# A Fourier mixing branch computed as even and odd halves, with the value projection moved ahead of it

## The chip, the cores and the metric

The kernel runs on one core of one Trainium2 chip. The metric is the device time of one execution in microseconds. The engines are named as the profile names them: PE is TensorE's matrix multiplication, PEld its weight load, DVE is VectorE, ACT is ScalarE, POOL is GpSimd and SP is SyncE, which issues most of the transfers here.

## The reference

The whole program is a hybrid mixer block, a cross attention and a feed-forward block, followed by a second block of two layers with adaptive norms. Everything is fp32, with 256 tokens of width 1024 (and 256 context tokens beside them). The change touches one place: the mixer of the first layer of the second block, which runs on both streams, x and context.

```python
def fourier_mix(a):                       # a: 256 tokens x 512
    a4 = a.reshape(b_, n, FOURIER_GROUPS, FOURIER_CH)     # 4 groups of 128 channels
    f = jnp.fft.fftn(a4, axes=(1, 3), norm="ortho").real  # over tokens and channels
    return f.reshape(b_, n, D_FOURIER)

def chunk_sgu(u, v, g_v, w_s, b_s):       # 4 groups of 128 channels, chunks of 128 tokens
    vh = rms_norm(v.reshape(b_, n, SGU_GROUPS, SGU_CH), g_v)
    vc = vh.reshape(b_, n // CHUNK_2, CHUNK_2, SGU_GROUPS, SGU_CH)
    mixed = jnp.einsum('hpq,bcqhd->bcphd', w_s, vc) + b_s.T[None, None, :, :, None]
    return u * mixed.reshape(b_, n, D_SGU)

def fourier_sgu_mixer(h, w_in, g_v, w_s, b_s, w_out):
    a, uv = jnp.split(h @ w_in, [D_FOURIER], axis=-1)
    u, v = jnp.split(jax.nn.gelu(uv), 2, axis=-1)
    return jnp.concatenate([fourier_mix(a), chunk_sgu(u, v, g_v, w_s, b_s)], axis=-1) @ w_out
```

## The kernel before, in words

The program is a chain of projections whose weights are streamed from memory, one chunk of at most 1 MB (128 partitions by 2048 numbers) at a time, in the order of a list called `plan`. SP loads chunks into three slots of `raw`. ACT copies a chunk to a reduced-precision `w_hi` (L234), DVE subtracts to get the rest `w_lo` (L242), and PE multiplies in three passes (L258, L259, L260), high by high, high by low and low by high. A chunk's loads and splits run two chunks ahead of PE. The activations are split in the same way into `xn_hi` and `xn_lo`. A second stream, 72 chunks of the adaptive norm's weights (`mods`), is multiplied by `mods_pe` (L1589) in places that a table, `MODS_BEHIND`, names; three of them (24 matmuls) belong to the stage of this change.

Both streams, 512 tokens, go through the branch together. Its projections are `ab_a` (the Fourier input), `ab_u` and `ab_v` (the gate and the value of the gating half), two chunks each, and then `ab_out`, four chunks. Between the last of the first three and `ab_out` lies what is called the Fourier stage here. It works on eight pieces j, one for each of four groups and two streams:

- `channels(j)` (L1731) multiplies by `dft_c`, cosine and minus sine side by side, 256 columns, two matmuls for the two halves of the tokens;
- ACT copies the 512 results to `mid` (L1772);
- four matmuls (L1743, L1744) multiply by the tokens' `dft_cos` and `dft_sin`, 256 columns each, into one sum;
- DVE copies the 256 results to `o_t` (L1811).

`channels(j + 1)` is issued ahead of the token matmuls of j. The value has to be normed before it is mixed over tokens: DVE squares and sums it (L1798, L1799), ACT makes a reciprocal root (L1767), DVE scales it (L1805, L1808), and PE mixes (L1749) after the eight pieces. Then come the three chunks of `mods`. Last, the branch's results are made ready for `ab_out`: the Fourier half is split by one ACT copy of 2048 numbers (L1774) and one DVE subtraction (L1815), the gated half is summed (L1823), multiplied (L1824) and split (L1778, L1815). `ab_out` starts when all of this but the last subtractions is done, by the line `pe.wait_ge(g_dve, 12)`. These are the waits ahead of the stage and in front of `ab_out`:

```python
            pe.wait_ge(evacuated, jobs["ab_v"].base + 2)
            ...
            pe.wait_ge(g_dve, 12)
            def branches_k(s, k):
                if s.c == 0 and k in (0, 4, 6):
                    pe.wait_ge(o_lo, max(1, k // 2))
```

All order on each engine is written out by hand, and engines wait for each other through counting semaphores.

Of the kernel before, what the change touches and what calls it, by code (L numbers as in the profile page):

```python
# [41 lines left out]
ACT = mybir.ActivationFunctionType  # L42
ALU = mybir.AluOpType
AX_X = mybir.AxisListType.X

P = 128
# [32 lines left out]
    "a1_down1": {0: (1, 1), 1: (1, 1), 2: (1, 1), 3: (1, 1), 5: (1, 1), 7: (3, 2)},  # L79
    "ab_v": {1: (3, 2)},  # L80
    "ab_out": {3: (3, 2)},
# [47 lines left out]
def build(nc, io, plan):  # L129
# [23 lines left out]
    with ExitStack() as ctx:  # L153
        def sb(name, shape, dt=F32, scope=ctx):
            return scope.enter_context(nc.sbuf_tensor(name, shape, dt))
# [105 lines left out]

        def pe_feature_major(pe, job, act_hi, act_lo, span, n_tiles=2, k_tiles=KT, before_k=None, after_chunk=None):


            for s in steps(job):
                bank_free(pe, s)
                pe.wait_ge(lo_ready, s.g + 1)
                for k in range(k_tiles):
                    if before_k is not None:
                        before_k(s, k)  # L270
                    for n in range(1 if packed(s) else n_tiles):
                        w = slice((n * k_tiles + k) * P, (n * k_tiles + k + 1) * P)
# [1435 lines left out]
        GATING = (4, 5, 0, 1)  # L1708
        o_t = area(0, KT, 2 * T)
# [7 lines left out]

        def branch_pe(pe, norm, turn):
            pe_feature_major(pe, jobs["ab_a"], xn_hi, xn_lo, XC, before_k=norm.ready_at_first(pe))
            turn()  # L1720
            pe_feature_major(pe, jobs["ab_u"], xn_hi, xn_lo, XC)
            pe_token_major(pe, jobs["ab_v"], XC)
            pe.wait_ge(evacuated, jobs["ab_v"].base + 2)
            pe.wait_ge(l0_tables_in, 16 * len(L0_TABLES))

            def channels(j):
                q, g = j // 4, j % 4
                if j >= 2:
                    pe.wait_ge(f_mid_out, j - 1)
                for nt in range(2):  # L1730
                    mm = pe.matmul(psum[:, j % 2, nt * T:(nt + 1) * T], a_t[:, g, q * T + nt * P:q * T + (nt + 1) * P], dft_c[:, :],  # L1731
                                   start=True, stop=True)
                mm.then_inc(f_mid, 1)

            channels(0)
            for j in range(8):
                if j + 1 < 8:
                    channels(j + 1)
                pe.wait_ge(f_mid_out, j + 1)
                if j >= 2:  # L1740
                    pe.wait_ge(f_sum_out, j - 1)
                for nt in range(2):
                    pe.matmul(psum[:, 2 + j % 2, 0:T], mid[j % 2][:, nt, 0:P], dft_cos[:, nt, :], start=(nt == 0), stop=False)  # L1743
                    mm = pe.matmul(psum[:, 2 + j % 2, 0:T], mid[j % 2][:, nt, P:T], dft_sin[:, nt, :], start=False, stop=(nt == 1))  # L1744
                mm.then_inc(f_sum, 1)
            pe.wait_ge(g_dve, 8)
            for tt in range(4):
                for g in range(4):
                    mm = pe.matmul(psum[:, GATING[g], tt * P:(tt + 1) * P], v_t[:, tt, g * P:(g + 1) * P], ws_t[:, g, :], start=True, stop=True)  # L1749
            mm.then_inc(g_pe, 1)  # L1750
            mods_pe(pe, mods_behind("ab_v", 1))
            pe.wait_ge(g_dve, 12)

            def branches_k(s, k):
                if s.c == 0 and k in (0, 4, 6):
                    pe.wait_ge(o_lo, max(1, k // 2))
            pe_feature_major(pe, jobs["ab_out"], xn_hi, xn_lo, XC, before_k=branches_k)

        def branch_act(act, norm, then):
            norm.act_rest(act)  # L1760
            for name in L0_TABLES:
                act.dma_start(L0_TABLES[name][:], io[name]).then_inc(l0_tables_in, 16)
            run_act(act, jobs["ab_a"], act_copy_to(act, a_t, w=2 * T), counts=True)
            run_act(act, jobs["ab_u"], act_copy_to(act, u_t, ACT.Gelu_apprx_tanh, w=2 * T), counts=True)
# [3 lines left out]
            for j in range(8):  # L1768
# [3 lines left out]
                act.activation(mid[j % 2], psum[:, j % 2, :].rearrange("p (n t) -> p n t", n=2), ACT.Copy).then_inc(f_mid_out, 1)  # L1772
            act.wait_ge(f_sum_out, 8)
            act.activation(xn_hi[:, 0:4, :], o_t[:, 0:4, :], ACT.Copy).then_inc(o_hi, 1)  # L1774
            for i in range(2):
                act.wait_ge(g_dve, 10 + 2 * i)
                k = slice(4 + 2 * i, 6 + 2 * i)
                act.activation(xn_hi[:, k, :], o_t[:, k, :], ACT.Copy).then_inc(o_hi, 1)  # L1778
            run_act(act, jobs["ab_out"], then.act_squares_after(act))

        def branch_dve(dve, norm, rows_out, columns):
# [3 lines left out]
            columns()  # L1785
            for name in ("ab_u", "ab_v"):
                run_dve(dve, jobs[name], None)
            n = 0
# [19 lines left out]
            o(dve.tensor_tensor(v4, v4, gv, ALU.mult))  # L1808
            for j in range(8):
                dve.wait_ge(f_sum, j + 1)  # L1810
                dve.tensor_copy(o_t[:, j % 4, (j // 4) * T:(j // 4 + 1) * T], psum[:, 2 + j % 2, 0:T]).then_inc(f_sum_out, 1)  # L1811
# [5 lines left out]
            low(0, slice(0, 4))  # L1817
            dve.wait_ge(g_pe, 1)
            for i in range(2):
                k = slice(4 + 2 * i, 6 + 2 * i)  # L1820
                gated = o_t[:, k, :].rearrange("p g (n t) -> p g n t", t=P)
                bs = bs_row[:, 2 * i:2 * i + 2, :].unsqueeze(2).to_broadcast([P, 2, 4, P])
                o(dve.tensor_tensor(gated, psum[:, GATING[2 * i]:GATING[2 * i] + 2, :].rearrange("p g (n t) -> p g n t", t=P), bs, ALU.add))  # L1823
                o(dve.tensor_tensor(o_t[:, k, :], o_t[:, k, :], u_t[:, 2 * i:2 * i + 2, :], ALU.mult))  # L1824
            for i in range(2):
                low(1 + i, slice(4 + 2 * i, 6 + 2 * i))
            run_dve(dve, jobs["ab_out"], dve_add_gated(dve, 2, gate_of(1), 2))
# [576 lines left out]
def shape_tables():  # L2404
# [218 lines left out]
```

## Time and profile before

| | |
|---|---|
| median of 3 runs | 2249.84 us (2249.29 to 2254.49) |
| the profiled execution's own time | 2254.1 us |
| its span | 2252.3 us |
| PE busy | 2133.1 us, 95% of the span |
| DVE, ACT, POOL busy | 1001.3, 791.9, 224.7 us |
| mean granted clock of PE | 0.982 of full |

An engine's busy time is that in which it executes something. The chain of waits is followed back from the last instruction, at each step to what released it. An fp32 matmul whose operands are not in reduced precision stands in the trace as two records, so the eight pieces' 32 token matmuls with `dft_cos` and `dft_sin` are 64 records. The record of a matmul begins before the one ahead of it has ended, since they are pipelined; the distance between two ends is the cost.

### The profile page before, as it was taken

The page shows a single profiled execution, that of the slowest core. Times are in us where ns is not written, and L with a number is a line of the kernel's source. Part 1 is how long each engine was busy: PE and PEld are TensorE (multiplying, and loading weights), DVE is VectorE, ACT ScalarE, POOL GpSimd, SP SyncE. Part 2 cuts the span into 40 slices and gives each one's busy share as a digit, 9 for nine tenths or more (in the row PEclk, how much of TensorE's full clock was granted, in tenths as well). Part 3 has the DMA queues.
Part 4 walks back from the last instruction along what each step waited for, and adds up shares of the span by engine and source line. Part 5 has one row for each costly group of instructions (what it writes and reads, how often), then busy time and mean ns, then how long its engine had stood idle before and what let it go on. Part 6 is the DMA issues. An engine that isn't in the chain of part 4 may idle for free.

```text
span 2252.3 us, 30888 instructions
## 1 busy us (share of the span) xinstructions
PE 2133.1 (95%) x13477; PEld 1809.1 (80%) x13477; DVE 1001.3 (44%) x1286; ACT 791.9 (35%) x969; POOL 224.7 (10%) x185
## 2 busy tenths in 40 slices
PE   6988998999999999999999999999999998989997
PEld 6985897999788888778768788877877886858997
DVE  6668554767522321353452232234223235645444
ACT  5642353555422222232232222233212223434443
POOL 1000000413111011100101101110100110001111
PEclk9999999999999999999999999999999999999999
DMA  6425454454531333451334332234234222363553
GB/s 227 150 77 211 166 185 187 152 185 161 196 144 65 112 128 115 171 199 57 112 134 165 103 112 85 83 129 165 107 133 159 82 78 98 113 242 135 175 178 104
DMA packets 53688, 314.23 MB, mean 140 GB/s; under 512 B 5936, under 2 KB 12081, under 8 KB 23729
## 3 DMA queue, kind: packets, MB, share of 16 engines
q1 hardware_dynamic: 51360, 309.51, 38.3%
q10 hardware_dynamic: 2192, 2.75, 0.4%
q8 instruction: 106, 1.74, 0.3%
q14 instruction: 30, 0.24, 0.0%
HBM read 311.19 MB, written 1.05 MB: 139 GB/s over the span
## 4 chain that ended last, share of the span: by engine, by line
PE 85%; DVE 9%; ACT 4%; issue 2%; DMA 1%; SPq 0%; DVEq 0%; ACTq 0%
PE psum L258 26%; PE psum L259 25%; PE psum L260 25%; PE psum L1589 2%; DVE w_lo L242 2%; ACT w_hi L234 2%; PE psum L1268 1%; PE psum L1246 1%; DVE work L407 1%; PE psum L1260 0%; PE psum L1743 0%; PE psum L1744 0%; DMA raw<-in_w_in_r 0%; DVE work L695 0%; ACT work L1280 0%
## 5 line engine op out<-in xcount | busy, mean ns | idle before, releaser
L258 PE MATMUL psum<-xn_hi,w_hi 128*128 128x256 f32 (+1 forms) x2504 | 849.1, 339 | 35.6 <-DVE xn_lo L416 15.7
L259 PE MATMUL psum<-xn_lo,w_hi 128*128 128x256 f32 (+1 forms) x2504 | 842.2, 336 | 0.0
L260 PE MATMUL psum<-xn_hi,w_lo 128*128 128x256 f32 (+1 forms) x2504 | 841.6, 336 | 0.0
L242 DVE TENSOR_TENSOR w_lo<-raw,w_hi 128x2048 fp32r<-128x2048 f32 (+1 forms) x246 | 509.9, 2073 | 420.2 <-ACT w_hi L234 419.4
L258 PEld LDWEIGHTS psum<-xn_hi,w_hi 128*128 128x128 f32 x2504 | 483.3, 193 | 99.1 <-issue 42.9
L260 PEld LDWEIGHTS psum<-xn_hi,w_lo 128*128 128x128 f32 x2504 | 482.8, 193 | 47.2
L259 PEld LDWEIGHTS psum<-xn_lo,w_hi 128*128 128x128 f32 x2504 | 483.2, 193 | 46.3 <-issue 0.7
L234 ACT ACTIVATE w_hi<-raw 128x2048 fp32r<-128x2048 f32 (+1 forms) x246 | 421.6, 1714 | 194.0 <-PE psum L260 157.2
L258 PE MATMUL psum<-h_hi,w_hi 128*128 128x512 f32 (+1 forms) x880 | 309.2, 351 | 1.7 <-POOL h_lo L1564 1.7
L259 PE MATMUL psum<-h_lo,w_hi 128*128 128x512 f32 (+1 forms) x880 | 307.7, 350 | 0.0
L260 PE MATMUL psum<-h_hi,w_lo 128*128 128x512 f32 (+1 forms) x880 | 307.7, 350 | 0.0
L1564 POOL TENSOR_TENSOR h_lo<-work,h_hi 128x512 fp32r<-128x512 f32 (+1 forms) x110 | 154.7, 1407 | 1171.9 <-ACT h_hi L1497 1171.9
L1535 DVE TENSOR_TENSOR work<-work,psum 128x512 f32<-128x512 f32 (+1 forms) x88 | 54.7, 621 | 407.7 <-ACT work L1486 407.7
L1486 ACT ACTIVATE work<-psum 128x512 f32<-128x512 f32 (+1 forms) x88 | 47.9, 544 | 514.4 <-PE psum L260 514.3
L258 PEld LDWEIGHTS psum<-h_hi,w_hi 128*128 128x128 f32 x880 | 165.5, 188 | 29.7 <-issue 4.1
L260 PEld LDWEIGHTS psum<-h_hi,w_lo 128*128 128x128 f32 x880 | 165.5, 188 | 23.9
L259 PEld LDWEIGHTS psum<-h_lo,w_hi 128*128 128x128 f32 x880 | 165.5, 188 | 23.5
L1421 DVE SCALAR_TENSOR_TENSOR xc<-psum,mods,xc 128x256 f32<-128x256 f32 x136 | 59.9, 480 | 235.1 <-PE psum L260 234.9
L343 POOL TENSOR_TENSOR work<-work 128x256 f32<-128x256 f32 (+1 forms) x60 | 62.2, 1037 | 763.2 <-ACT work L334 712.8
L334 ACT ACTIVATE work<-xc 128x512 f32<-128x512 f32 (+2 forms) x48 | 30.3, 632 | 228.8 <-DVE xc L1421 202.3
L1589 PE MATMUL psum<-raw,c_pad 128*32 128x256 f32 x1152 | 77.9, 391 | 11.7 <-DMA raw<-in_mod 11.7
L1497 ACT ACTIVATE h_hi<-work 128x512 fp32r<-128x512 f32 (+1 forms) x110 | 60.1, 547 | 78.7 <-DVE work L1535 78.7
(341 smaller groups left out, 1321.8 us busy)
## 6 DMA issues: line engine op xcount, KB each, us to landing
raw<-in_mod SPq DMA_DIRECT2D x72, 1024.0 KB, 4.8
raw<-in_a_up SPq DMA_DIRECT2D x42, 1024.0 KB, 4.8
raw<-in_b_up SPq DMA_DIRECT2D x42, 1024.0 KB, 4.8
raw<-in_ffn_up SPq DMA_DIRECT2D x22, 1024.0 KB, 5.1
raw<-in_a_down SPq DMA_DIRECT2D x32, 704.0 KB, 4.1
raw<-in_b_down SPq DMA_DIRECT2D x32, 704.0 KB, 4.2
raw<-in_ffn_down SPq DMA_DIRECT2D x16, 704.0 KB, 4.1
raw<-in_wo SPq DMA_DIRECT2D x8, 1024.0 KB, 4.8
```

What stands on the lines that cost most here:

```text
L234: act.activation(w_hi[:, slot, 0:size], raw[:, raw_slot(("main", g)), 0:size], ACT.Copy).then_inc(hi_ready, 1)
L242: dve.tensor_tensor(w_lo[:, slot, 0:size], raw[:, raw_slot(("main", g)), 0:size], w_hi[:, slot, 0:size].bitcast(F32), ALU.subtract).then_i ...
L258: pe.matmul(out, lh, rh, start=first, stop=False, skip_group_check=group)
L259: pe.matmul(out, lh, rl, start=False, stop=False, skip_group_check=group)
L260: return pe.matmul(out, ll, rh, start=False, stop=last, skip_group_check=group)
L343: pool.tensor_tensor(nrm[:, 0, 0:self.w], nrm[:, 0, 0:self.w], nrm[:, k, 0:self.w], ALU.add).then_inc(n_added, 1)
L1421: mm = dve.scalar_tensor_tensor(x, got, gate[:, tile, h], x, ALU.mult, ALU.add)
L1486: act.activation(b[r, 0, 0:self.w], psum[r, s.bank, 0:self.w], ACT.Silu).then_inc(ff_gate, 1)
L1497: act.activation(out, b[r, 1:2, 0:self.w], ACT.Copy).then_inc(ff_hi, 1)
L1535: dve.tensor_tensor(b[r, 1, 0:self.w], b[r, 0, 0:self.w], up[up_r], ALU.mult).then_inc(evacuated, 1)
L1564: pool.tensor_tensor(lo, b[r, 1:2, 0:self.w], hi.bitcast(F32), ALU.subtract).then_inc(ff_lo, 1)
L1589: mm = pe.matmul(psum[q, 7, 0:256], c_pad[:, k, C_AT - 2 * j:C_AT - 2 * j + 32], raw[:, raw_slot(("mod", m)), k * 256:(k + 1) * 256], star ...
```

## The change

The Fourier transform of real input is symmetric. The change computes half of each transform and makes the other half from it.

- Over channels, only the cosines of 0 to 64 and the sines of 1 to 63 are multiplied, 128 columns for 256. ACT makes both full rows of `mid` from them with four activations for the one of before: the cosine half, the sine half, and the mirror image of each, written with a step of -1 (the sine's with scale -1).
- Over tokens, cosine and sine sums are kept apart, 129 columns each for 256. ACT copies the sine sum to SBUF (`odd_out`), and DVE writes sum and difference of the two (`halves`), the difference with a step of -1 in output and ascending input.
- `ab_v` is projected ahead of `ab_u`, so the value's norm is computed beside `ab_u`'s matmuls. PE no longer waits for the last evacuation of the projections before the stage, only for the one before it.
- The gating matmuls are cut in two parts of 8 (after pieces 1 and 4) and the three `mods` chunks are put singly after pieces 2, 4 and 6.
- The split of the results is cut from three groups to six (each Fourier group as it comes), and `ab_out` takes its k tiles in the order 0, 1, 4, 5, 2, 6, 7, 3, each waiting only for its own.

```diff
@@ pe_feature_major
-                for k in range(k_tiles):
+                for k in k_order:
@@ tables
+        GATED_BANK, MID_BANK, TOKEN_BANK = 0, 2, 4
+        OUT_ORDER = (0, 1, 4, 5, 2, 6, 7, 3)
+        OUT_READY = {0: 1, 1: 2, 4: 3, 2: 4, 6: 5, 3: 6}
@@ branch_pe
+            pe_token_major(pe, jobs["ab_v"], XC)
             pe_feature_major(pe, jobs["ab_u"], xn_hi, xn_lo, XC)
-            pe_token_major(pe, jobs["ab_v"], XC)
-            pe.wait_ge(evacuated, jobs["ab_v"].base + 2)
+            pe.wait_ge(evacuated, jobs["ab_u"].base + 1)
...
+            def tokens(j):
+                pe.wait_ge(f_mid_out, j + 1)
+                if j >= 2:
+                    pe.wait_ge(f_sum_out, 2 * j - 2)
+                for nt in range(2):
+                    pe.matmul(psum[:, TOKEN_BANK + j % 2, 0:P + 1], mid[j % 2][:, nt, 0:P], dft_cos[:, nt, :], start=(nt == 0), stop=(nt == 1))
+                for nt in range(2):
+                    mm = pe.matmul(psum[:, TOKEN_BANK + j % 2, T:T + P + 1], mid[j % 2][:, nt, P:T], dft_sin[:, nt, :], start=(nt == 0), stop=(nt == 1))
+                mm.then_inc(f_sum, 1)
...
             for j in range(8):
                 if j + 1 < 8:
                     channels(j + 1)
+                tokens(j)
+                if j == 1:
+                    gating(0)
+                if j == 4:
+                    gating(1)
+                if j in (2, 4, 6):
+                    mods_pe(pe, 1)
@@ branch_act
+            def middle(j):
+                act.wait_ge(f_mid, j + 1)
+                if j >= 2:
+                    act.wait_ge(f_sum, j - 1)
+                got, m, h = psum[:, MID_BANK + j % 2, 0:T].rearrange("p (n t) -> p n t", n=2), mid[j % 2], P // 2
+                act.activation(m[:, :, 0:h + 1], got[:, :, 0:h + 1], ACT.Copy)
+                act.activation(m[:, :, P + 1:P + h], got[:, :, h + 1:P], ACT.Copy)
+                act.activation(m[:, :, P - 1:h:-1], got[:, :, 1:h], ACT.Copy)
+                act.activation(m[:, :, 2 * P - 1:P + h:-1], got[:, :, h + 1:P], ACT.Copy, scale=-1.0).then_inc(f_mid_out, 1)
...
+            def odd_out(j):
+                act.wait_ge(f_sum, j + 1)
...
+                act.activation(odd_half[j % 2], psum[:, TOKEN_BANK + j % 2, T:T + P + 1], ACT.Copy).then_inc(f_odd, 1)
...
+            middle(0)
+            for j in range(3):
+                middle(j + 1)
+                odd_out(j)
+            fourier_high(0)
@@ branch_dve
+            def halves(j):
+                dve.wait_ge(f_odd, j + 1)
+                g, t = j // 2, j % 2 * T
+                even, odd = psum[:, TOKEN_BANK + j % 2, 0:P + 1], odd_half[j % 2]
+                dve.tensor_tensor(o_t[:, g, t:t + P + 1], even, odd, ALU.add).then_inc(f_sum_out, 1)
+                dve.tensor_tensor(o_t[:, g, t + T - 1:t + P:-1], even[:, 1:P], odd[:, 1:P], ALU.subtract).then_inc(f_sum_out, 1)
```

On PE, at the start of the Fourier stage, this is what stood there before: two `channels`, then four token matmuls and two channel matmuls for each piece, all with 256 columns, and at the end the gating and the `mods` in one block each.

```order
L1731 MATMUL psum<-dft_c,a_t 128x256 x4
L1743 MATMUL psum<-dft_cos,work 128x256
L1744 MATMUL psum<-dft_sin,work 128x256
L1743 MATMUL psum<-dft_cos,work 128x256
L1744 MATMUL psum<-dft_sin,work 128x256
...
L1749 MATMUL psum<-ws_t,v_t 128x128 x16
L1589 MATMUL psum<-raw,c_pad 32x256 x24
L258 MATMUL psum<-xn_hi,w_hi 128x512
```

On PE the stage of the changed kernel begins as follows; L1735 is `channels`, L1744 and L1746 are `tokens`, L1756 is `gating`.

```order
L1735 MATMUL psum<-dft_c,a_t 128x128 x4
L1744 MATMUL psum<-dft_cos,work 128x129 x2
L1746 MATMUL psum<-dft_sin,work 128x129 x2
L1735 MATMUL psum<-dft_c,a_t 128x128 x2
L1744 MATMUL psum<-dft_cos,work 128x129 x2
L1746 MATMUL psum<-dft_sin,work 128x129 x2
L1756 MATMUL psum<-ws_t,v_t 128x128 x8
L1735 MATMUL psum<-dft_c,a_t 128x128 x2
L1744 MATMUL psum<-dft_cos,work 128x129 x2
L1746 MATMUL psum<-dft_sin,work 128x129 x2
L1589 MATMUL psum<-raw,c_pad 32x256 x8
```

The matmuls are as many as before but half as wide, and half of the gating and a `mods` chunk have moved in between pieces.

On ACT, around the same place, these rows stood before: the last evacuations of the projections (L1393 is u, L1405 is v), the root of the norm, the eight copies of the middle, and the splits.

```order
L1393 ACTIVATE u_t<-psum 128x1024
L234 ACTIVATE w_hi<-raw 128x2048
L1405 ACTIVATE v_t<-psum 128x4x256
L234 ACTIVATE w_hi<-raw 128x2048
L1405 ACTIVATE v_t<-psum 128x4x256
L1767 ACT_TABLE_LOAD
L1767 ACTIVATE work<-work 128x16
L1772 ACTIVATE work<-psum 128x512 x8
L1774 ACTIVATE xn_hi<-work 128x2048
```

And these stand there on ACT in the changed kernel, down to the first `odd_out` (L1811).

```order
L1405 ACTIVATE v_t<-psum 128x4x256
L1785 ACT_TABLE_LOAD
L1785 ACTIVATE work<-work 128x16
L234 ACTIVATE w_hi<-raw 128x2048
L1393 ACT_TABLE_LOAD
L1393 ACTIVATE u_t<-psum 128x1024
L234 ACTIVATE w_hi<-raw 128x2048
L1393 ACTIVATE u_t<-psum 128x1024
L1793 ACTIVATE work<-psum 128x2x65
L1794 ACTIVATE work<-psum 128x2x63
L1795 ACTIVATE work<-psum 128x2x63
L1796 ACTIVATE work<-psum 128x2x63
```

The root and its table load have moved ahead of the evacuation of u, one more table load stands before that evacuation, and one more stands at the next norm (ahead of L361), since the root's table is no longer the last one loaded.

## Rows read from the trace of the kernel before

**Rows 1.** The page: span, busy shares, and the chain that ended last, by engine.

```profile
span 2252.3 us, 30888 instructions
PE 2133.1 (95%) x13477; PEld 1809.1 (80%) x13477; DVE 1001.3 (44%) x1286; ACT 791.9 (35%) x969; POOL 224.7 (10%) x185
PE 85%; DVE 9%; ACT 4%; issue 2%; DMA 1%; SPq 0%; DVEq 0%; ACTq 0%
```

**Rows 2.** Stretches of time: length, busy us of each engine, granted clock, DMA.

```profile
1047.40:1085.80 38.40, 30.26 (x177) 25.12 (x176) 20.36 (x21) 10.05 (x13) 0.00 (x0) 0.91 0.10 37
1053.00:1059.70 6.70, 5.51 (x13) 4.38 (x14) 5.90 (x8) 1.19 (x3) 0.00 (x0) 0.50 0.00 0
1059.70:1076.00 16.30, 16.30 (x77) 14.34 (x77) 2.55 (x6) 3.58 (x6) 0.00 (x0) 1.00 0.00 1
1085.80:1091.00 5.20, 5.17 (x16) 4.10 (x17) 4.65 (x3) 2.87 (x2) 0.00 (x0) 0.67 0.80 336
```

**Rows 3.** PE in order of time: start, us, line, count, idle time before.

```profile
1047.15 0.28 PE L260 MATMUL psum<-w_hi,xn_lo 128*128 128x256 f32 x1
1048.60 1.99 PE L1731 MATMUL psum<-dft_c,a_t 128*128 128x256 f32 x8 [1.17 <-ACT v_t L1405]
1054.19 1.22 PE L1743 MATMUL psum<-dft_cos,work 128*128 128x256 f32 x2 [3.60 <-ACT work L1772]
...
1079.63 2.80 PE L1589 MATMUL psum<-raw,c_pad 128*32 128x256 f32 x48
1085.83 0.50 PE L258 MATMUL psum<-xn_hi,w_hi 128*128 128x512 f32 x1 [3.40 <-DVE work L1824]
```

**Rows 4.** The chain of waits, in order of time: start, us, what.

```profile
1061.45 0.86 PE psum L1731 x4
1062.32 0.43 PE psum L1743 x2
```

**Rows 5.** The gating matmuls' line: count, ns, first and last start.

```profile
L1749 PE MATMUL psum<-ws_t,v_t x32: 273/275/275, 1076.0 to 1079.4; 128*128 128x128 f32 x32
```

**Rows 6.** ACT in order of time, from the last projection to the splits.

```profile
1047.53 1.02 ACT L1405 ACTIVATE v_t<-psum 128x1024 f32<-128x1024 f32 x1 [8.69 <-PE psum L260]
1048.57 1.28 ACT L1767 ACT_TABLE_LOAD   x1
1053.44 0.22 ACT L1767 ACTIVATE work<-work 128x16 f32<-128x16 f32 x1 [3.59 <-DVE work L1800]
1053.56 1.07 ACT L1772 ACTIVATE work<-psum 128x512 f32<-128x512 f32 x2
1076.63 1.91 ACT L1774 ACTIVATE xn_hi<-work 128x2048 fp32r<-128x2048 f32 x1 [3.32 <-DVE work L1811]
```

**Rows 7.** Groups by line and shape, ACT copies from PSUM and small DVE operations.

```profile
L1486 ACT ACTIVATE work<-psum 128x256 f32<-128x256 f32 x21 | 8.1, 385 | 56.2 <-PE psum L260 56.2
L1772 ACT ACTIVATE work<-psum 128x512 f32<-128x512 f32 x8 | 4.7, 594 | 15.1 <-PE psum L1731 15.1
L791 DVE COPY s<-psum 128x128 f32<-128x128 f32 x1 | 0.3, 284 | 0.0
```

**Rows 8.** DVE in order of time, in the stage and after it.

```profile
1048.58 2.29 DVE L1798 TENSOR_TENSOR work<-v_t 128x2048 f32<-128x2048 f32 x1 [7.42 <-ACT v_t L1405]
...
1056.72 2.29 DVE L1808 TENSOR_TENSOR v_t<-v_t,gv_row 128x2048 f32<-128x2048 f32 x1
...
1076.17 0.42 DVE L1811 COPY work<-psum 128x256 f32<-128x256 f32 x1 [1.30 <-PE psum L1744]
1098.74 1.66 DVE L1421 SCALAR_TENSOR_TENSOR xc<-psum,mods,xc 128x256 f32<-128x256 f32 x4 [7.74 <-PE psum L260]
1109.61 1.66 DVE L1421 SCALAR_TENSOR_TENSOR xc<-psum,mods,xc 128x256 f32<-128x256 f32 x4 [3.98 <-PE psum L260]
```

**Rows 9.** ACT in order of time, at the norm behind `ab_out`.

```profile
1133.06 1.06 ACT L334 ACTIVATE work<-xc 128x1024 f32<-128x1024 f32 x1 [8.01 <-DVE xc L1421]
1138.19 0.63 ACT L363 ACTIVATE rstd<-mean 128x512 f32<-128x512 f32 x1 [3.98 <-DVE mean L384]
```

More of the change, by code:

```diff
@@ L79 @@
     "a1_down1": {0: (1, 1), 1: (1, 1), 2: (1, 1), 3: (1, 1), 5: (1, 1), 7: (3, 2)},
-    "ab_v": {1: (3, 2)},
+    "ab_u": {1: (3, 2)},
     "ab_out": {3: (3, 2)},
@@ L1707, in build @@
         L0_TABLES = dict(dft_c=dft_c, dft_cos=dft_cos, dft_sin=dft_sin, ws_t=ws_t, bs_row=bs_row, gv_row=gv_row)
-        GATING = (4, 5, 0, 1)
+        GATED_BANK, MID_BANK, TOKEN_BANK = 0, 2, 4
+        odd_half = [work[:, 5120 + i * T:5120 + i * T + P + 1] for i in range(2)]
+        f_odd, f_clear = sem("fourier_odd_half"), sem("fourier_zeros")
+        OUT_ORDER = (0, 1, 4, 5, 2, 6, 7, 3)
+        OUT_READY = {0: 1, 1: 2, 4: 3, 2: 4, 6: 5, 3: 6}
         o_t = area(0, KT, 2 * T)
@@ L1730, in channels, with gating @@
                 for nt in range(2):
-                    mm = pe.matmul(psum[:, j % 2, nt * T:(nt + 1) * T], a_t[:, g, q * T + nt * P:q * T + (nt + 1) * P], dft_c[:, :],
+                    mm = pe.matmul(psum[:, MID_BANK + j % 2, nt * P:(nt + 1) * P], a_t[:, g, q * T + nt * P:q * T + (nt + 1) * P], dft_c[:, :],
                                    start=True, stop=True)
                 mm.then_inc(f_mid, 1)
+            def tokens(j):
[7 more added lines that the diff above has]
+                mm.then_inc(f_sum, 1)
+            def gating(i):
+                if i == 0:
+                    pe.wait_ge(evacuated, jobs["ab_u"].base + 2)
+                pe.wait_ge(g_dve, 8 + i)
+                for tt in range(4):
+                    for g in range(2):
+                        w = 2 * i + g
+                        mm = pe.matmul(psum[:, GATED_BANK + g, tt * P:(tt + 1) * P], v_t[:, tt, w * P:(w + 1) * P], ws_t[:, w, :],
+                                       start=True, stop=True)
+                mm.then_inc(g_pe, 1)
+            pe.wait_ge(f_clear, 2)
             channels(0)
@@ L1738, in branch_pe @@
                     channels(j + 1)
[L1739 to L1752, printed above, removed]
+                tokens(j)
[5 more added lines that the diff above has]
+                    mods_pe(pe, 1)
             def branches_k(s, k):
-                if s.c == 0 and k in (0, 4, 6):
-                    pe.wait_ge(o_lo, max(1, k // 2))
-            pe_feature_major(pe, jobs["ab_out"], xn_hi, xn_lo, XC, before_k=branches_k)
+                if s.c == 0 and k in OUT_READY:
+                    pe.wait_ge(o_lo, OUT_READY[k])
+            pe_feature_major(pe, jobs["ab_out"], xn_hi, xn_lo, XC, before_k=branches_k, k_order=OUT_ORDER)
         def branch_act(act, norm, then):
@@ L1767, in branch_act @@
             act.activation(vst2, vst, ACT.Abs_reciprocal_sqrt).then_inc(g_act, 1)
-            for j in range(8):
+            run_act(act, jobs["ab_u"], act_copy_to(act, u_t, ACT.Gelu_apprx_tanh, w=2 * T), counts=True)
+            def middle(j):
                 act.wait_ge(f_mid, j + 1)
@@ L1771, in branch_act, with fourier_high, gated_high @@
                     act.wait_ge(f_sum, j - 1)
[L1772 to L1775, printed above, removed]
+                got, m, h = psum[:, MID_BANK + j % 2, 0:T].rearrange("p (n t) -> p n t", n=2), mid[j % 2], P // 2
[3 more added lines that the diff above has]
+                act.activation(m[:, :, 2 * P - 1:P + h:-1], got[:, :, h + 1:P], ACT.Copy, scale=-1.0).then_inc(f_mid_out, 1)
+            def fourier_high(g):
+                act.wait_ge(f_sum_out, 4 * g + 4)
+                act.activation(xn_hi[:, g, :], o_t[:, g, :], ACT.Copy).then_inc(o_hi, 1)
+            def gated_high(i):
                 act.wait_ge(g_dve, 10 + 2 * i)
@@ L1785, in branch_dve @@
             columns()
-            for name in ("ab_u", "ab_v"):
-                run_dve(dve, jobs[name], None)
+            run_dve(dve, jobs["ab_v"], None)
             n = 0
@@ L1808, in branch_dve @@
             o(dve.tensor_tensor(v4, v4, gv, ALU.mult))
-            for j in range(8):
-                dve.wait_ge(f_sum, j + 1)
-                dve.tensor_copy(o_t[:, j % 4, (j // 4) * T:(j // 4 + 1) * T], psum[:, 2 + j % 2, 0:T]).then_inc(f_sum_out, 1)
+            for i in range(2):
+                dve.memset(mid[i][:, :, P:2 * P:P // 2], 0.0).then_inc(f_clear, 1)
+            run_dve(dve, jobs["ab_u"], None)
+            def halves(j):
[4 more added lines that the diff above has]
+                dve.tensor_tensor(o_t[:, g, t + T - 1:t + P:-1], even[:, 1:P], odd[:, 1:P], ALU.subtract).then_inc(f_sum_out, 1)
             def low(i, k):
@@ L2613, in feed @@
         return jobs
-    plan += feed("ffn") + feed("a1") + [("ab_a", 2, full), ("ab_u", 2, full), ("ab_v", 2, full), ("ab_out", 4, full)]
+    plan += feed("ffn") + feed("a1") + [("ab_a", 2, full), ("ab_v", 2, full), ("ab_u", 2, full), ("ab_out", 4, full)]
     plan += feed("a2") + feed("b1") + [("k2", 1, full), ("q2", 4, full), ("v2", 1, full), ("wo2", 4, full)]
```

65 lines of the change are left out of this document (48 added, 17 removed).

## The prediction

> **What bounds the kernel now.** I read the page first. PE is busy for 95% of the span, and the chain that ended last lies on PE for 85% [rows 1]. So only two things move the time: PE work taken away, and PE waits taken away. Next I looked at PE between the last matmul of the projections, which ends at 1047.4, and the first of `ab_out` at 1085.8 [rows 3]. This Fourier stage takes 38.4 us, 1.7% of the span, with PE busy 30.3 us of it at a mean granted clock of 0.91 [rows 2]. The order of PE's rows shows three waits: 1.17 us for the evacuation of v, 3.60 us for ACT's copy of the first piece, and 3.40 us for the last gated product on DVE [rows 3]. The second has a cause that the ACT rows show. The table load and the root of the norm stand ahead of the copies, and the root waits for DVE's square and sum, so the first copy starts only at 1053.56 [rows 6]. After these waits the clock is low. From 1053.0 to 1059.7 it is 0.50 of full, that is 1.2 GHz, and then 1.00, 2.4 GHz [rows 2].
>
> The stage adds up. At full clock a matmul of 256 fp32 columns costs 0.43 us (two records in 0.43, four in 0.86) [rows 4]. There are 16 of `channels` and 32 for the tokens, 48 x 0.43 = 20.6 us. A gating matmul of 128 columns costs two records at (1079.4 - 1076.0) / 31 = 0.11 us each, 0.22 us [rows 5], and 16 of them 3.5 us. The `mods` block is 2.8 us [rows 3]. Work is thus 26.9 us and the waits are 8.2 us. The 13 records run at half clock [rows 2] lose 13 x 0.21 = 2.8 us. That gives 37.9, and 0.5 us are left for three restarts of an empty PE.
>
> One more cost hangs on the last wait. `ab_out`'s first chunk is evacuated at 1098.74 and the second at 1109.61 [rows 8]. A chunk takes 10.87 us, but the first took 12.91 us from its start at 1085.83. The 2.0 us more are the restart (0.50 us for the first matmul) [rows 3] and a clock of 0.67 over 5.2 us [rows 2].
>
> **The change part by part.** *PE work.* 48 matmuls go from 256 columns to 128 or 129. The nearest row is gating, fp32 with 128 columns and a new weight for each: 0.22 us [rows 5]. 48 x 0.22 = 10.6 us, so 10 us less. Gating and `mods` stay at 3.5 + 2.8 us. PE work is then 16.9 us. No row shows an odd count of columns. Its cost lies between 0.22 and the 0.43 of 256 columns; I take 0.22, since 129 is one column from the row, and the other end for the 32 token matmuls would be 6.7 us more.
>
> *The front.* PE no longer waits for the last evacuation. It is released by the one before it, 11 us old. ACT evacuates u (1.02 us, as v now [rows 6]) and goes straight to the first copy, since the norm of v lies beside `ab_u`. That norm occupies DVE from v's evacuation for 10.4 us (1048.58 to 1056.72 + 2.29) [rows 8]. v's last chunk now ends one projection, about 22 us, earlier, near 1025.5, so DVE is free near 1037. It then has the two `w_lo` splits of `ab_out` to make, of the same 2048 numbers as L1808, 2.29 us each. The second follows the second `w_hi`, which ACT makes after it has evacuated u's first chunk (1036.3 + 1.28 for the table + 1.0 + 1.9 = 1040.5), and ends near 1043. The stage begins at 1047.4, so about 4 us of cover hide the whole norm. The root's wait on ACT also lies there. Cost nothing.
>
> *ACT's copies.* Four activations of 126 or 130 numbers and one of 129 take the place of one with 512. From PSUM, 256 numbers take 385 ns and 512 take 594 ns [rows 7], hence 0.82 ns a number and 0.18 us fixed: 0.28 us for such a piece. Two copies in a row took 1.07 us for 2 x 0.59 [rows 6, 7], so the next begins 0.11 us before the last has ended, and a piece adds 0.17 us. The four take 3 x 0.17 + 0.28 = 0.8 us, and `odd_out` 0.2 to 0.3 us more. No row shows a write with a step of -1. The bounds are nothing extra (every copy here costs by its count alone) and, from the spread of rows, the whole of a 256-number copy for each reversed piece, 0.1 us more; a step that took each number singly is a rival, below.
>
> The Trainium skill (ScalarE: Activation LUTs, What ACT_TABLE_LOAD costs) gives 186 ns + 0.833 ns a number, with 93 ns of overlap. This rule, which speaks against cutting a copy in four, makes the four 0.89 us for my 0.80, and the stage 0.1 us longer. The rows here decide, and agree within 0.1 us.
>
> *How the pieces follow each other.* `channels(0)` ends 0.44 us into the stage and `channels(1)` at 0.88. ACT is free at 1.0, its four pieces end at 1.75, and PE, idle 0.9 us, starts the tokens of piece 0. The restart costs 0.27 us (0.50 against 0.23 for a matmul of 512 in three-pass form, which is 10.87 / 48) [rows 3, 8]. From there ACT has, between the end of `channels(j + 1)` and the tokens that need it, one block of tokens and one of channels on PE, 0.88 + 0.44 = 1.32 us, against 0.8 us. Each piece also brings DVE two operations. A 128-number one takes 0.28 us [rows 7], together 0.5 us. The larger copies, 0.6 us for a Fourier group (512) and 1.0 us for a gated pair (1024), stand beside a gating part (1.76 us) or a `mods` chunk (0.93 us). Laying the four queues out piece by piece with these durations, I find no further wait on PE. The narrowest places are the copies of piece 7, 0.3 us ahead of PE, and k tiles 4 and 5 of `ab_out`, ready at 20.1 us and reached at 20.5. Stage: 16.9 + 0.9 + 0.3 = 18.0 us.
>
> *The tail.* Before, copy, split, sum and product stood one after another from 1076.17 [rows 8] to 1085.83. Now Fourier tiles 0 and 1 are split by 16 us, and PE's own first 5.5 us of `ab_out` hide the rest. If that cover were gone, 3 us of DVE and ACT work would show.
>
> *Table loads.* One more stands at the evacuation of u (hidden above) and one at the next norm. There ACT waits 3.98 us for DVE [rows 9], and a load takes 1.28 us [rows 6]. Nothing; without that wait, 1.3 us.
>
> *Sum.* Stage 38.4 - 18.0 = 20.4 us, and in `ab_out`'s first chunk 2.0 us, since PE neither restarts nor, after such short waits, should lose its clock. 22.4 us in all. The profiled execution of 2254.1 us would be 2231.7. That execution is 4.3 us over the median of the three runs, and at the upper end of their spread, so I take the same 22.4 us off the median: 2227.4 us.
>
> **The rivals.** *A, small pieces are dear* (chance 0.15). If each reversed copy costs 0.5 us more, ACT falls behind at each piece, and my layout gives a stage of 21.7 us and 2231 us. With 1.0 us it is 27.7 us and 2237 us. For it: 16 such instructions, none in the trace. Against it: ACT and DVE rows cost by their count of numbers. The odd column counts, at 6.7 us more, would give 2234 us.
>
> *B, the clock falls in the stage* (0.10). A stretch like that of before, 6.7 us at 0.50 [rows 2], costs 3.3 us: 2231 us. The whole stage at 1.2 GHz makes 16.9 into 33.7 us, and with `ab_out`'s 2.0 us lost again 2245 us. Against it: the low stretch came behind 1.17 and 3.60 us of idle time, and from 1059.7 to 1076.0 the same kind of matmuls ran at 1.00. The skill (TensorE: Matmul & The Clock Gate, The HAM clock gate) says that the half rate is the idle state and sustained activity ends it; by that rule the stage keeps 2.4 GHz, as these rows have it.
>
> *C, the gain comes but is lost later* (0.04), in a wait for weights or in a low clock at the next norm. Loads are released by buffers as PE uses them, so they come earlier too. It would give 2240 to 2250 us.
>
> *D, it does not do what it says* (0.04): the norm of v delays DVE's splits of `ab_out` past 1047.4, and PE gets the old wait back at the first k tile. It decides when DVE is 4 us later than I count, and each us more costs one. The old 3.6 + 3.4 us of waits would give 2234 us.
>
> *E, slower* (0.02). One mechanism: a reversed copy moves its numbers one at a time, on ACT's path. The layout passes 40 us of stage when each reversed copy takes 1.9 us more, and the time is then over 2250 us; at 2.5 us more it is 2260 us. That is 15 ns a number against 0.82 measured, so I leave it 0.02.
>
> **How the numbers follow.** The forecast, 2227.4 us, has 0.65; its own range is 2222 to 2232, from runs that spread over 5 us and from 1 or 2 us of handovers that I did not count. The range of 2221 to 2239 takes in A up to 1.0 us, the odd columns, B's short stretch and D. It leaves out C, B's worst case and E, and a part of A. What can be told from no change is about 0.3%, 6.8 us. Faster by more, under 2243 us: 0.95, all but B's worst case, half of C and E. Within 0.3%: 0.03. Slower: 0.02.
>
> **What would show it.** In the trace of the changed kernel the L1735, L1744 and L1746 matmuls should be 0.11 us apart by record. The stage should take 18 us, with one wait near 0.9 us for L1796. The clock should stay 1.00 from 1048 to 1080, and `ab_out`'s first chunk should take 11 us. L1795 and L1796 should take 0.28 us as L1793 does. The prediction is wrong if L1795 or L1796 take more than 0.5 us, if the L1744 records are over 0.15 us apart, if PE waits at L258 with k tile 4, or if the norm behind `ab_out` starts late.

## The result, and the profile after

| | before | changed |
|---|---|---|
| first set of runs, median | 2251.16 us (4 runs) | 2225.69 us (4 runs, 2224.19 to 2231.78) |
| second set, median | 2249.71 us (15 runs, 2245.11 to 2254.49) | 2229.28 us (4 runs, 2228.22 to 2231.57) |
| profiled span | 2252.3 us | 2222.4 us |

The ratio of the first set is 0.989 with a 95% interval of 0.9868 to 0.9913, and that of the second 0.9905, 0.9888 to 0.9922. The eight runs of the changed kernel have a median of 2228.3 us. That is 21.4 us under the 2249.7 of the second set's before; 2227.4 us, 22.4 us less, was forecast.

The page of the changed kernel (span, busy shares, the chain by engine) answers to [rows 1]. PE's busy time has fallen by 21.6 us, 12.1 us of it in the stage (30.26 to 18.14 us), and its share of the chain is the same: the kernel is bound by PE as it was.

```profile
span 2222.4 us, 30946 instructions
PE 2111.5 (95%) x13477; PEld 1790.4 (81%) x13477; DVE 1001.0 (45%) x1299; ACT 798.1 (36%) x1006; POOL 224.3 (10%) x185
PE 85%; DVE 8%; ACT 3%; issue 2%; DMA 1%; SPq 0%; DVEq 0%; ACTq 0%
```

The stretches of the changed kernel, the Fourier stage and then the first chunk of `ab_out` (length, busy us of PE, PEld, DVE, ACT and POOL, granted clock, DMA), answer to [rows 2].

```profile
1040.10:1059.20 19.10, 18.14 (x178) 15.84 (x177) 8.30 (x20) 11.29 (x44) 0.00 (x0) 1.00 0.33 112
1059.20:1070.30 11.10, 11.10 (x51) 9.16 (x50) 7.12 (x9) 3.79 (x4) 0.00 (x0) 1.00 0.52 180
```

The stage takes 19.1 us for 38.4, at a full clock throughout. PE in order of time, beginning with the first matmuls of the stage, answers to [rows 3].

```profile
1039.98 1.05 PE L1735 MATMUL psum<-dft_c,a_t 128*128 128x128 f32 x8
1041.99 0.71 PE L1744 MATMUL psum<-dft_cos,work 128*128 128x129 f32 x4 [0.96 <-ACT work L1796]
...
1046.56 0.61 PE L1744 MATMUL psum<-dft_cos,work 128*128 128x129 f32 x4
1047.01 0.61 PE L1746 MATMUL psum<-dft_sin,work 128*128 128x129 f32 x4
1047.55 1.07 PE L1589 MATMUL psum<-raw,c_pad 128*32 128x256 f32 x16
1048.55 0.71 PE L1735 MATMUL psum<-dft_c,a_t 128*128 128x128 f32 x4
1049.10 0.61 PE L1744 MATMUL psum<-dft_cos,work 128*128 128x129 f32 x4
...
1059.00 0.48 PE L258 MATMUL psum<-xn_hi,w_hi 128*128 128x512 f32 x1
```

There is one wait, 0.96 us. Four records of 129 columns begin 0.45 us before the next four, 0.11 us each. Around a `mods` chunk the distances are longer, 0.54 and 0.55 us for 0.45, which comes back below. `ab_out` begins with no wait.

ACT in the same stage, and at the norm behind `ab_out`, answers to [rows 6, 9]. L1793 and L1794 write forward, L1795 and L1796 with a step of -1.

```profile
1040.24 1.02 ACT L1393 ACTIVATE u_t<-psum 128x1024 f32<-128x1024 f32 x1 [6.78 <-PE psum L260]
1041.16 0.28 ACT L1793 ACTIVATE work<-psum 128x130 f32<-128x130 f32 x1
1041.32 0.28 ACT L1794 ACTIVATE work<-psum 128x126 f32<-128x126 f32 x1
1041.47 0.30 ACT L1795 ACTIVATE work<-psum 128x126 f32<-128x126 f32 x1
1041.63 0.31 ACT L1796 ACTIVATE work<-psum 128x126 f32<-128x126 f32 x1
...
1104.60 1.06 ACT L334 ACTIVATE work<-xc 128x1024 f32<-128x1024 f32 x1 [8.01 <-DVE xc L1421]
1105.67 1.28 ACT L361 ACT_TABLE_LOAD   x1
1106.97 0.20 ACT L361 ACTIVATE small<-small 128x1 f32<-128x1 f32 x1
1109.09 0.63 ACT L363 ACTIVATE rstd<-mean 128x512 f32<-128x512 f32 x1 [1.92 <-DVE mean L384]
```

The four copies take 0.78 us. The reversed ones begin at the same distance as the others. The added table load lies in what was a wait of 3.98 us, of which 1.92 us are left.

DVE in order of time: the end of the value's norm, the last split of a chunk ahead of the stage, the first `halves` (L1870, and L1871 with a step of -1), and the evacuation of `ab_out`'s first chunk. It answers to [rows 8].

```profile
1027.65 2.29 DVE L1860 TENSOR_TENSOR v_t<-v_t,gv_row 128x2048 f32<-128x2048 f32 x1
...
1033.50 2.29 DVE L242 TENSOR_TENSOR w_lo<-raw,w_hi 128x2048 fp32r<-128x2048 f32 x1 [1.22 <-ACT w_hi L234]
1043.50 0.29 DVE L1870 TENSOR_TENSOR work<-psum,work 128x129 f32<-128x129 f32 x1 [7.71 <-ACT work L1811]
1043.71 0.28 DVE L1871 TENSOR_TENSOR work<-psum,work 128x127 f32<-128x127 f32 x1
...
1070.28 1.66 DVE L1421 SCALAR_TENSOR_TENSOR xc<-psum,mods,xc 128x256 f32<-128x256 f32 x4 [3.77 <-PE psum L260]
```

**A measure for the branch alone.** The profiled spans are 29.9 us apart, more than any set of medians. Part of that lies ahead of the branch, in code that is the same. The root of the branch's own norm started at these times in the kernel before, the changed kernel, and the changed kernel once more.

```profile
973.08 0.63 ACT L363 ACTIVATE rstd<-mean 128x512 f32<-128x512 f32 x1 [0.66 <-DVE mean L384]
```

```profile
965.71 0.63 ACT L363 ACTIVATE rstd<-mean 128x512 f32<-128x512 f32 x1 [0.66 <-DVE mean L384]
```

```profile
971.74 0.63 ACT L363 ACTIVATE rstd<-mean 128x512 f32<-128x512 f32 x1 [0.66 <-DVE mean L384]
```

So the experiments are read by the distance D from this row to the first evacuation of `ab_out` (the first L1421 behind it). Before it is 1098.74 - 973.08 = 125.7 us, changed 1070.28 - 965.71 = 104.6 us, a gain of 21.1 us. Behind the branch, from the root of the next norm to the last one, the two kernels take 1103.8 and 1103.0 us. Between the end of D and that next root lie three more chunks of `ab_out`, 32.6 us in both, and the norm's own matmuls (L350), here before and then changed.

```profile
1134.17 3.25 PE L350 MATMUL psum<-work,ones 128*128 128x512 f32 x4 [2.05 <-ACT work L334]
```

```profile
1105.71 2.62 PE L350 MATMUL psum<-work,ones 128*128 128x512 f32 x4 [2.05 <-ACT work L334]
```

D leaves these out. From its end to the next root the two kernels take 39.5 and 38.8 us, and the kernels below between 38.2 and 39.9 us. From root to root the gain is thus 21.7 us. Nothing is given back.

### The profile page after: what moved, and what is told of

Same layout as the page of the kernel before. It is cut to its first block, busy times and chain, and to the rows that moved or that the text cites. A ratio compares the mean times of both kernels' runs of the same rounds, so it can differ in the third digit from the quotient of the medians.

```text
span 2222.4 us, 30946 instructions
## 1 busy us (share of the span) xinstructions
PE 2111.5 (95%) x13477; PEld 1790.4 (81%) x13477; DVE 1001.0 (45%) x1299; ACT 798.1 (36%) x1006; POOL 224.3 (10%) x185
## 3 DMA queue, kind: packets, MB, share of 16 engines
q1 hardware_dynamic: 51360, 309.51, 38.8%
## 4 chain that ended last, share of the span: by engine, by line
PE 85%; DVE 8%; ACT 3%; issue 2%; DMA 1%; SPq 0%; DVEq 0%; ACTq 0%
PE psum L258 26%; PE psum L259 25%; PE psum L260 25%; PE psum L1589 2%; DVE w_lo L242 2%; ACT w_hi L234 2%; PE psum L1268 1%; DMA raw<-in_mod 1%; PE psum L1246 1%; DVE work L407 1%; PE psum L1260 0%; DMA raw<-in_w_in_r 0%; DVE work L695 0%; ACT work L1280 0%; PE psum L871 0%
## 5 line engine op out<-in xcount | busy, mean ns | idle before, releaser
L1421 DVE SCALAR_TENSOR_TENSOR xc<-psum,mods,xc 128x256 f32<-128x256 f32 x136 | 59.9, 479 | 230.5 <-PE psum L260 230.4
L1589 PE MATMUL psum<-raw,c_pad 128*32 128x256 f32 x1152 | 79.3, 395 | 13.6 <-DMA raw<-in_mod 13.6
```

The lines of the kernel that those rows point to most:

```text
L1421: mm = dve.scalar_tensor_tensor(x, got, gate[:, tile, h], x, ALU.mult, ALU.add)
L1589: mm = pe.matmul(psum[q, 7, 0:256], c_pad[:, k, C_AT - 2 * j:C_AT - 2 * j + 32], raw[:, raw_slot(("mod", m)), k * 256:(k + 1) * 256], star ...
```

## The experiments

| kernel | median, us | ratio to before, 95% interval | D, us |
|---|---|---|---|
| before | 2249.71 | | 125.7 |
| the change again | 2229.28 | 0.9905 (0.9888 to 0.9922) | 104.4 |
| ab_v last again | 2239.16 | 0.9945 (0.9928 to 0.9963) | 112.3 |
| ab_v first alone | 2246.21 | 0.9977 (0.9965 to 0.9989) | 119.2 |
| full width again | 2234.55 | 0.9928 (0.9911 to 0.9944) | 113.5 |
| mods in one block | 2226.72 | 0.9899 (0.9875 to 0.9922) | 103.8 |
| a mods chunk first | 2225.32 | 0.9885 (0.9867 to 0.9903) | 102.9 |
| the old tail | 2236.71 | 0.9933 (0.9914 to 0.9952) | 109.5 |

The last three ran on another chip than the four ahead of them, beside a before of 2252.54 us (7 runs, 2246.96 to 2254.82). Each D comes from one profile; the changed kernel's two are 0.1 us apart.

**The change again.** No edit.

> The changed kernel once more, unaltered. Theory (stage): the change is worth what its own place shows, 19.3 us in the Fourier stage (38.4 to 19.1 us) and 2.0 us in the first chunk of ab_out, 21 to 22 us in all, 2229 to 2230 us against a before of 2251 us; the 8 us more that the two profiled spans are apart came from stretches of low clock that fell elsewhere in unchanged code, and will come out differently this time. So the root of the norm ahead of the branch (L363), whose code is the same in both kernels, will start at a third time, neither 973.1 us nor 965.7 us, or at one of the two by chance, and the stage will again take 19.1 us. Rival (hidden effect): the change makes the part ahead of the branch faster too, by some effect of placement; then that root starts again near 965.7 us and the medians are 29 us apart.

The stage and the chunk behind it took the same time to 0.1 us (D 104.4), while the root ahead of the branch started 6 us later than in the first profile, and 1.3 us earlier than in the kernel before. So the 7 us by which the first two profiles differ there are no gain of the change; one of about 1 us ahead of the branch can't be excluded by single profiles. What moved is the clock. The work between the roots of two earlier norms is the same in all of them. In the kernel before, in the changed kernel and in the changed kernel once more it stood as follows.

```profile
376.77:456.25 79.48, 74.47 (x604) 71.33 (x595) 55.42 (x86) 44.40 (x70) 25.56 (x14) 0.96 0.47 169
```

```profile
373.51:450.42 76.91, 71.78 (x603) 69.34 (x594) 55.40 (x86) 44.35 (x69) 25.55 (x14) 1.00 0.49 175
```

```profile
375.45:454.86 79.41, 74.47 (x603) 71.33 (x594) 55.42 (x86) 44.37 (x69) 25.55 (x14) 0.96 0.48 170
```

The same 603 matmul records took 76.9 us at a granted clock of 1.00 and 79.4 us at 0.96, in one and the same program. In the profiles of the other experiments this stretch took 79.3 to 79.5 us in the three that ran on this chip, and 76.7 us in the three on the other. Whether the chip decides it or chance was not tried.

**ab_v last again.** The changed kernel with the projections in the order of before.

```diff
-            pe_token_major(pe, jobs["ab_v"], XC)
             pe_feature_major(pe, jobs["ab_u"], xn_hi, xn_lo, XC)
-            pe.wait_ge(evacuated, jobs["ab_u"].base + 1)
+            pe_token_major(pe, jobs["ab_v"], XC)
+            pe.wait_ge(evacuated, jobs["ab_v"].base + 1)
```

ACT's and DVE's parts, `plan` and the table follow; the two memsets stand ahead of the norm.

> The changed kernel with ab_u projected first and ab_v second, as before the change; its norm lies in front of the stage again. Theory: the waits ahead of the first tokens come back. Laying out the queues, PE waits 6 us for the first tokens (ACT's copies stand behind the root, which waits 4.9 us for DVE), 2 us for the first gating part and about 0.5 us more; the stage is 26 us at full clock, and up to 29 us if the clock falls to half behind these waits. So 7 to 10 us slower than the changed kernel, 2233 to 2238 us. Rival (width is all): the order of the projections is worth under 2 us once the matmuls are half as wide, since the first copies are short; 2226 to 2229 us.

PE in this kernel, and its granted clock from 1053.3 to 1060.0 (columns as above):

```profile
1047.29 1.05 PE L1735 MATMUL psum<-dft_c,a_t 128*128 128x128 f32 x8
1054.40 1.23 PE L1744 MATMUL psum<-dft_cos,work 128*128 128x129 f32 x4 [6.05 <-ACT work L1796]
...
1074.13 0.48 PE L258 MATMUL psum<-xn_hi,w_hi 128*128 128x512 f32 x1
```

```profile
1053.30:1060.00 6.70, 5.49 (x25) 5.22 (x26) 6.12 (x10) 2.89 (x15) 0.00 (x0) 0.53 0.00 0
```

The wait of 6 us is there and the clock falls behind it. The stage is 26.8 us, and D 7.8 us longer than in the changed kernel: 5.1 us more of waiting (6.05 for 0.96), and 2.7 us that the low clock took. The expected wait of 2 us for gating did not show: at half clock PE reached it at 1059.2, when DVE had just finished the norm of v. The median, 2239.2 us, is 1 us over the expected 2233 to 2238, and 9.9 us over the changed kernel's. Of the 2.1 us that D doesn't hold, 1.1 us lie between its end and the next root in the two profiles (39.8 us for 38.7); the rest is within the scatter of the runs.

**ab_v first alone.** The kernel before with this edit and what follows from it.

```diff
-            pe_feature_major(pe, jobs["ab_u"], xn_hi, xn_lo, XC)
             pe_token_major(pe, jobs["ab_v"], XC)
-            pe.wait_ge(evacuated, jobs["ab_v"].base + 2)
+            pe_feature_major(pe, jobs["ab_u"], xn_hi, xn_lo, XC)
+            pe.wait_ge(evacuated, jobs["ab_u"].base + 2)
```

> The kernel before with one part of the change alone: ab_v ahead of ab_u, and its norm beside ab_u's matmuls. Full transforms, one block of gating and mods, the splits as before. Theory: of the waits 1.17, 3.60 and 3.40 us only the second goes, and with it the stretch at half clock behind it (2.8 us). Stage 38.4 - 3.6 - 2.8 - 0.2 = 31.8 us, and the 2.0 us in ab_out's first chunk stay. 6.6 us faster than before, about 2244 us. Rival: the clock falls anyway behind the 1.17 us wait, and the gain is only 3.6 us, 2247 us.

```profile
1047.15 1.99 PE L1731 MATMUL psum<-dft_c,a_t 128*128 128x256 f32 x8 [1.17 <-ACT u_t L1393]
1048.98 0.69 PE L1743 MATMUL psum<-dft_cos,work 128*128 128x256 f32 x2
...
1077.92 0.50 PE L258 MATMUL psum<-xn_hi,w_hi 128*128 128x512 f32 x1 [3.40 <-DVE work L1824]
```

```profile
1047.00:1078.00 31.00, 27.45 (x177) 23.33 (x177) 10.59 (x14) 7.94 (x12) 0.00 (x0) 1.00 0.13 48
```

PE's rows show the first and the last wait of before unchanged and the second gone, and the granted clock is 1.00 over the whole stage. D is 6.5 us shorter, where 6.6 were expected: 3.6 us of waiting and 2.8 us of half clock. The rival, in which the clock falls behind the 1.17 us wait too, falls. The medians are 3.5 us apart, with 2.5 to 7.9 us inside the interval. So the branch's own distance decides here, not the median.

**Full width again.** The changed kernel with the transforms of before.

```diff
-                for nt in range(2):
-                    pe.matmul(psum[:, TOKEN_BANK + j % 2, 0:P + 1], mid[j % 2][:, nt, 0:P], dft_cos[:, nt, :], start=(nt == 0), stop=(nt == 1))
-                for nt in range(2):
-                    mm = pe.matmul(psum[:, TOKEN_BANK + j % 2, T:T + P + 1], mid[j % 2][:, nt, P:T], dft_sin[:, nt, :], start=(nt == 0), stop=(nt == 1))
+                for nt in range(2):
+                    pe.matmul(psum[:, TOKEN_BANK + j % 2, 0:T], mid[j % 2][:, nt, 0:P], dft_cos[:, nt, :], start=(nt == 0), stop=False)
+                    mm = pe.matmul(psum[:, TOKEN_BANK + j % 2, 0:T], mid[j % 2][:, nt, P:T], dft_sin[:, nt, :], start=False, stop=(nt == 1))
```

`channels`, the tables, and the copies on ACT (one of 512 for the four) and on DVE (one of 256 for the two halves) follow; `odd_out` does nothing.

> The changed kernel with the full transforms of before: channels 256 columns, tokens 256 columns into one sum, one ACT copy of 512 a piece and one DVE copy of 256, with the new order of projections, gating, mods and splits. Theory: PE work in the stage goes back up by 48 x 0.21 = 10 us and the 0.96 us wait for the first tokens goes, since the first copy is one of 0.6 us; the stage is 28 us, 9 us longer than the changed kernel's, at full clock. 2234 to 2236 us. Rival (order is nothing without width, or the reverse): if it comes out within 2 us of the changed kernel, the width was hidden and the order did it all; if near 2245 us, the order is worth little.

```profile
1043.27 1.89 PE L1735 MATMUL psum<-dft_c,a_t 128*128 128x256 f32 x8
1045.09 0.70 PE L1744 MATMUL psum<-dft_cos,work 128*128 128x256 f32 x2
...
1071.17 0.58 PE L258 MATMUL psum<-xn_hi,w_hi 128*128 128x512 f32 x1
```

D is 113.5 us, 9.0 us longer than in the changed kernel, and the median of 2234.6 us lies in the expected 2234 to 2236. PE has no wait in the stage: the work has grown by 10 us, and the wait for the first tokens, 0.96 us, is gone.

**Mods in one block.** `mods_pe(pe, 3)` after piece 6, for one chunk each after 2, 4 and 6.

> The changed kernel with its three mods chunks in one block after piece 6, for one each after pieces 2, 4 and 6. From the root ahead of the branch (L363) to the first evacuation of ab_out (L1421) the changed kernel takes 104.5 us. Theory (switching): each change between the full matmuls and the mods' 32-column ones costs PE 0.1 us, six of them in the changed kernel and two here; so 104.1 us. Rival: the 0.1 us belong to each wait for a landed chunk, and stay at three; 104.5 us. In the median of runs neither can be told from 2229 us.

PE in this kernel:

```profile
1055.49 0.61 PE L1746 MATMUL psum<-dft_sin,work 128*128 128x129 f32 x4
1056.03 2.80 PE L1589 MATMUL psum<-raw,c_pad 128*32 128x256 f32 x48
1058.76 0.71 PE L1744 MATMUL psum<-dft_cos,work 128*128 128x129 f32 x4
1059.31 0.61 PE L1746 MATMUL psum<-dft_sin,work 128*128 128x129 f32 x4
```

D is 103.8 us, 0.7 us less, more than the 0.4 us expected. The three chunks now take 1059.31 - 1055.49 - 0.45 - 0.45 = 2.9 us with both switches. A single one took 1049.10 - 1047.01 - 0.45 - 0.45 = 1.2 us, three of them 3.6 us. The rival, in which the cost belongs to each chunk's own wait, falls. The distances at the four switches that are gone make up 0.4 us, as the theory had it. The other 0.3 us lie in the chunks themselves: 1.00 us from the start of a single one to the next record, 2.73 us for the three together. Why is not shown.

**A mods chunk first.**

```diff
+                if j == 0:
+                    mods_pe(pe, 1)
                 tokens(j)
...
-                if j in (2, 4, 6):
-                    mods_pe(pe, 1)
+                if j == 6:
+                    mods_pe(pe, 2)
```

> The changed kernel with one mods chunk between channels(1) and the tokens of piece 0, and the other two in one block after piece 6. Theory: the 0.96 us in which PE waits for ACT's first copies is filled by a chunk of 0.93 us that has to be done anyway, and two switches fewer save 0.2 us. PE has no wait left in the stage: 17.8 us for 19.1 us, 103.2 us from L363 to L1421 for 104.5, with every later group of splits still ahead of PE by 0.3 us or more. Rival (cover gone): moving the chunks takes the cover from the gated pair's ACT copy, and PE waits as long at the tokens of piece 7 as it gained at piece 0; 104.3 us or more. Median 2228 us, inside the noise of 2229 us.

```profile
1041.60 1.05 PE L1735 MATMUL psum<-dft_c,a_t 128*128 128x128 f32 x8
1042.58 1.07 PE L1589 MATMUL psum<-raw,c_pad 128*32 128x256 f32 x16
1043.61 0.71 PE L1744 MATMUL psum<-dft_cos,work 128*128 128x129 f32 x4
```

PE goes from channels to `mods` to tokens without a wait. D is 102.9 us, where 103.2 were expected, 1.6 us under the changed kernel, and no new wait shows at piece 7. This version has the lowest median of all, 2225.3 us. Against the changed kernel the medians can't tell it apart (0.9885 against 0.9905, with overlapping intervals); the profile does.

**The old tail.** Half transforms and v first, but the end of the stage as before.

```diff
+            gating(0)
+            gating(1)
+            mods_pe(pe, 3)
+            pe.wait_ge(g_dve, 12)
...
-            pe_feature_major(pe, jobs["ab_out"], xn_hi, xn_lo, XC, before_k=branches_k, k_order=OUT_ORDER)
+            pe_feature_major(pe, jobs["ab_out"], xn_hi, xn_lo, XC, before_k=branches_k)
```

The waits of `branches_k` are those of before, and ACT and DVE split the results in three groups again, behind the last piece.

> The changed kernel with half transforms and v first, but gating in one block after the eight pieces, mods in one block after it, and the results split in three groups with the old wait for the last product and the old order of k. Theory: PE's work is the same, but the last copy, the split of 2048 numbers (1.9 + 2.3 us) and two sums and two products (4 x 1.25 us) stand one after another behind the last tokens again: PE waits 3.4 to 3.6 us before ab_out, which starts 22.0 us into the stage, and its first chunk takes 12.9 us at the lowered clock. From L363 to L1421 109.4 us for 104.5; median 2233 to 2235 us. Rival: with half as much PE work ahead of it the tail is caught by gating and mods (6.6 us of work), and costs under 1 us; 105.5 us.

```profile
1053.87 3.74 PE L1756 MATMUL psum<-ws_t,v_t 128*128 128x128 f32 x32
1057.54 2.80 PE L1589 MATMUL psum<-raw,c_pad 128*32 128x256 f32 x48
1064.11 0.50 PE L258 MATMUL psum<-xn_hi,w_hi 128*128 128x512 f32 x1 [3.78 <-DVE work L1878]
```

```profile
1064.10:1069.30 5.20, 5.19 (x16) 4.16 (x17) 4.65 (x3) 2.85 (x2) 0.00 (x0) 0.67 0.73 304
```

The wait in front of `ab_out` is back, 3.78 us, and the clock behind it is low, 0.67 over 5.2 us as in the kernel before. D is 109.5 us where 109.4 were expected. The rival falls: from the end of the tokens to `ab_out` it is 1064.11 - 1053.87 = 10.2 us, and gating and `mods` cover 6.4 us of it.

**What each part is worth.** Undone one at a time in the changed kernel, by D against 104.5 us, the order of the projections gives 7.8 us, the width 9.0 us, and the tail with its interleaving 5.0 us. Their sum of 21.8 us is close to the 21.1 us of all together. By this measure the parts hardly lean on each other, though each figure comes from one profile, and the tail's from another chip.

## Why the prediction was right

*The bound.* It was PE's work and waits in one stage, as read. No change upstream or downstream shows beyond the clock's own scatter.

*Width.* 10 us less were forecast for 48 half-width matmuls. Full width again cost 9.0 us: the 10 us, less the wait for the first tokens, which wide transforms don't have. The odd count of columns costs nothing: 129 columns run at the 0.11 us a record of 128.

*The front.* The norm of v and both splits ended at 1035.8, 4.3 us ahead of the stage, where about 4 were forecast. Rival D fell by that row, and the part's worth, 6.5 us with its half clock, is shown alone.

*ACT's copies.* 0.8 us were forecast for four, 0.78 us measured. Rival A and rival E fell together: a reversed copy costs no more than a forward one. The fixed cost that the Trainium skill gives (ScalarE: Activation LUTs, What ACT_TABLE_LOAD costs) would have made them 0.89 us; the trace has less.

*The clock.* 1.00 in the stage, as forecast, and the chunk behind it took 11.1 us for 12.9. That the long waits bring the low clock back is shown by the two kernels in which they return. Behind 6.05 us of waiting the clock was 0.53, and behind 3.78 us it was 0.67; the chunk there took 1076.99 - 1064.11 = 12.9 us again. Behind a single wait of 0.96 us, or of 1.17 us in `ab_v` first alone, it stayed at 1.00. Rival B fell.

*The term that was off.* The stage, 18.0 us forecast, took 19.1 us. I had taken a `mods` chunk at 0.93 us, a third of the block of before, and left out what putting it between full-size matmuls costs. Each takes 1.2 us there, 0.8 us more for the three. The one-block kernel got 0.7 us of that back. The rest, some 0.2 us, is in 128 records at 0.112 us (16 gating records in 1.79 us) for my 0.11. The first chunk of `ab_out` gave 1.8 us for the 2.0 forecast. So stage and chunk together gave 21.1 us where I had 22.4.

*The tail.* The laid-out queues had k tiles 4 and 5 ready 0.4 us before PE needs them. PE did not wait. The table load at the next norm was hidden, as forecast; rival C fell by the equal times behind the branch.

The first set of medians, 25.5 us apart, would have made the gain look larger than the branch can give. The second, 20.4 us apart, and the eight runs taken together agree with D's 21.1 us. That the first median of the changed kernel, 2225.7 us, lies only 1.7 us from the forecast is in part luck: the gain was smaller than forecast, and the one of those runs that was profiled was faster in unchanged code.

## What to carry to other kernels

Where PE is bound and one stage has short work with long waits, lay out that stage's queues by hand from rows of the trace, piece by piece. It gave each part here to within about 1 us, and it shows which work already in the program can fill a wait. Symmetric transforms can be halved if another engine with room makes the mirror image. Measure a gain of 1% by the distance between two rows around the edit, since in the profiles here the clock in unchanged code moved the row ahead of the branch by as much as 7 us.

## What the runs showed of the hardware

- Writing with a step of -1 cost nothing more on ACT (0.27 to 0.36 us for 126 numbers, forward or reversed, 0.16 us after the one ahead) and on DVE (0.28 us for 127, 0.29 us for 129 forward).
- Changing between 128-column and 32-column weights took PE about 0.1 us each way, by the distances of records (0.54 and 0.55 us for 0.45).
- A table load on ACT took 1.28 us, and the next activation began 1.30 us after the load (1105.67 to 1106.97). I had allowed no more, and the Trainium skill (ScalarE: Activation LUTs, What ACT_TABLE_LOAD costs) names 2.66 us for a switch. Here the load and nothing else stood between the activations.
- Four short copies in a row began 0.16 us apart, each recorded as 0.28 to 0.31 us long. I had worked out 0.17 us.
- Two profiles of one program differ by 6 us in unchanged code (965.7 and 971.7), and nine profiles of programs that are the same up to the branch by 7 us, with a granted clock of 0.96 or 1.00 over the same matmuls. What decides when the low stretches fall was not tried.
